# Scaling the compressed branch's weights one head later, and turning them behind the next head's weights

## What is computed

```python
s_c = einsum('bghqd,bgcd->bghqc', qb, k_cmp) + dense_bias(d_c)   # compressed branch
p_c = masked_softmax(s_c, d_c >= 0)                               # 15 weights a query
o_c = einsum('bghqc,bgcd->bghqd', p_c, v_cmp)
# the selected and the window branch have the same form over the 256 keys: o_s, o_w
o = stack([o_c, o_s, o_w])
y = sum(gates[..., None] * o * silu(z), axis=2)                   # over the 3 branches
out = y.reshape(Bn, T, B_WIDTH) @ out_w
```

## Time and profile before

| what | us |
| --- | --- |
| median of 3 runs | 1065.21 |
| lowest and highest of them | 1064.49, 1065.55 |
| the profiled execution, its own time | 1068.07 |
| its span, first to last instruction | 1066.3 |
| TensorE busy in the span | 1024.5 (96%) |
| VectorE busy | 689.1 (65%) |
| ScalarE busy | 624.1 (59%) |
| GpSimd busy | 126.2 (12%) |
| mean granted TensorE clock | 0.994 |

### The profile page before, as it was taken

How to read it: one execution, slowest core, us unless ns; L and a number is a source line. 1 busy time by engine, 2 the same in 40 slices (tenths; PEclk the granted TensorE clock), 3 DMA queues, 4 the chain that set the end, 5 groups by cost and what they waited for, 6 DMA issues and landing times. The chain is left out here.

```text
span 1066.3 us, 16886 instructions
## 1 busy us (share of the span) xinstructions
PE 1024.5 (96%) x6975; PEld 920.6 (86%) x6975; DVE 689.1 (65%) x980; ACT 624.1 (59%) x954; POOL 126.2 (12%) x119
## 2 busy tenths in 40 slices
PE   6999998999999999999999999999999989999997
PEld 5999897988998888689888799999889869899995
DVE  5788676857865687776566564545557876545454
ACT  6679676655664666365666654344456975443443
POOL 1010048440200122530000100000000100000000
PEclk9999999999999999899999999999999999999999
DMA  9885255443677432246332465565544355655540
GB/s 337 301 256 169 77 160 197 150 128 92 198 244 269 159 119 80 80 133 213 129 119 81 137 216 177 182 196 182 177 155 159 122 175 178 196 177 182 196 159 40
DMA packets 117500, 178.41 MB, mean 167 GB/s; under 512 B 5204, under 2 KB 74098, under 8 KB 117424
## 3 DMA queue, kind: packets, MB, share of 16 engines
q1 hardware_dynamic: 116160, 174.23, 50.0%
q0 software_dynamic: 1120, 2.97, 0.8%
q10 hardware_dynamic: 144, 0.13, 0.0%
HBM read 176.27 MB, written 1.05 MB: 166 GB/s over the span
## 5 line engine op out<-in xcount | busy, mean ns | idle before, releaser
L1481 DVE TENSOR_TENSOR sb_w_lo<-sb_raw,sb_w_hi 128x2048 fp32r<-128x2048 f32 (+1 forms) x139 | 309.5, 2227 | 202.1 <-ACT sb_w_hi L775 202.0
L775 ACT ACTIVATE sb_w_hi<-sb_raw 128x2048 fp32r<-128x2048 f32 (+1 forms) x135 | 256.2, 1900 | 136.4 <-PE G L2319 106.3
L2317 PE MATMUL X<-sb_hT_hi,sb_w_hi 128*128 128x256 f32 x784 | 223.2, 285 | 2.6 <-DVE sb_hT_lo L1843 1.1
L2318 PE MATMUL X<-sb_hT_lo,sb_w_hi 128*128 128x256 f32 x784 | 221.3, 282 | 0.0
L2319 PE MATMUL X<-sb_hT_hi,sb_w_lo 128*128 128x256 f32 x784 | 221.2, 282 | 0.0
L2317 PEld LDWEIGHTS X<-sb_hT_hi,sb_w_hi 128*128 128x128 f32 x784 | 149.3, 190 | 5.4 <-DVE sb_w_lo L1481 2.2
L2318 PEld LDWEIGHTS X<-sb_hT_lo,sb_w_hi 128*128 128x128 f32 x784 | 149.4, 191 | 0.7
L2319 PEld LDWEIGHTS X<-sb_hT_hi,sb_w_lo 128*128 128x128 f32 x784 | 149.4, 191 | 0.0
L2317 PE MATMUL G<-sb_w_hi,sb_uT_hi 128*128 128x512 f32 x304 | 121.4, 399 | 4.8 <-DVE sb_uT_lo L2257 4.8
L2319 PE MATMUL G<-sb_w_hi,sb_uT_lo 128*128 128x512 f32 x304 | 120.6, 397 | 0.0
L2318 PE MATMUL G<-sb_w_lo,sb_uT_hi 128*128 128x512 f32 x304 | 120.5, 396 | 0.0
(11 more groups left out here) (507 smaller groups left out, 1970.7 us busy)
## 6 DMA issues: line engine op xcount, KB each, us to landing
sb_raw<-in_mlp_w SPq DMA_DIRECT2D x64, 1024.0 KB, 5.2
sb_raw<-in_ada_w SPq DMA_DIRECT2D x22, 1024.0 KB, 5.3
sb_raw<-in_b_in_w SPq DMA_DIRECT2D x16, 1024.0 KB, 5.7
sb_raw<-in_a_in_w SPq DMA_DIRECT2D x14, 1024.0 KB, 7.0
sb_raw<-in_sb_w_qkv SPq DMA_DIRECT2D x12, 1024.0 KB, 5.2
sb_raw<-in_rg_w_in SPq DMA_DIRECT2D x8, 1024.0 KB, 5.3
sb_raw<-in_a_out_w SPq DMA_DIRECT2D x4, 1024.0 KB, 5.1
sb_raw<-in_b_out_w SPq DMA_DIRECT2D x4, 1024.0 KB, 5.3
```

The costliest lines, as they stand in the source:

```text
L775: nc.scalar.activation(split_tile(w_hi, m)[:, 0:nk * w], raw_of(b)[:, 0:nk * w], ACT.Copy).then_inc(S["w_hi"], 1)
L1481: ins = nc.vector.tensor_tensor(split_tile(w_lo, m)[:, at], raw_of(b)[:, at], split_tile(w_hi, m)[:, at].bitcast(F32), ALU.subtract)
L2317: dt32(out, lh, rh, start=first, stop=False, skip_group_check=shared)
L2318: dt32(out, lh, rl, start=False, stop=False, skip_group_check=shared)
```

## The change

It moves two calls. On VectorE `c_scale()` goes from head 10, behind `scores(12)`, to head 11, behind that head's copy and `z_silu` and ahead of `scores(13)`. On TensorE `c_weights_T()` goes from head 11, behind `scores(13)` and ahead of `head_out(11)`, to head 12, right behind `weights_T(12)` and ahead of `scores(14)`. No instruction is added or removed, and ScalarE's, GpSimd's and SyncE's lists stay as they are.

```diff
--- before.py
+++ after.py
@@ -2049,10 +2049,10 @@
                 nc.vector.tensor_copy(pT[h % 2][:, 1, :], TB[1][:, 0:384]).then_inc(S["pT1"], 1)
                 if h in Z_TILES:
                     z_silu(2 + Z_TILES.index(h))
+                if h == 11:
+                    c_scale()
                 if h + 2 < BH:
                     scores(h + 2)
-                if h == 10:
-                    c_scale()
                 if h in Z_SPLITS:
                     split_for(first_mm["b_z"] + 6 + Z_SPLITS.index(h))
                 if h >= 2 and h % 2 == 0:
@@ -3042,6 +3042,8 @@
             piece = 0
             for h in range(BH):
                 weights_T(h)
+                if h == 12:
+                    c_weights_T()
                 for i in range((Z_PIECES[h] + 1) // 2):
                     z_piece(piece)
                     piece += 1
@@ -3050,8 +3052,6 @@
                 for i in range(Z_PIECES[h] // 2):
                     z_piece(piece)
                     piece += 1
-                if h == 11:
-                    c_weights_T()
                 if h in (12, 13):
                     c_out(h - 12)
                 if h == BH - 1:
```

## The result

The changed kernel takes **1070.23 us** (median of 4 launches, 1068.42 to 1071.02) against 1065.38 before: a ratio of 1.0039, 95% interval 1.0027 to 1.0050. It is slower by 4 to 5 us: the medians are 4.9 apart, the ratio stands for 4.2. I had forecast 1065.8 and a range up to 1067.2; the result lies outside it, on the side of the rival that I had given 0.05.

The account below looks back on a forecast made before the run. It took nmx(13) on VectorE, releasing `scores(14)`, `head_exp(13)` and then `c_out(0)`, to bound the stretch. All terms were 0 except 0.6 us from the port, with the clock unchanged: 1065.8 on the median 1065.21, range 1063.7 to 1067.2.

Parts of the forecast that it names:

- Part 1: VectorE, head 10: with `c_scale` gone, `head_out(11)` on TensorE begins 2.15 us earlier, worth 0 at the end.
- Part 2: VectorE, head 11: `c_scale` enters at 425.78; the work ahead of nmx(13) is the same, in itself 0.
- Part 3: VectorE against GpSimd: L2011 runs into L716, L595 is pushed behind it, and nmx(13) comes 0.6 us late.
- rival C: VectorE against GpSimd: both `c_scale` products lose to L716 and L595, nmx(13) 1.4 us late, 1066.6; chance 0.18.
- Parts 4 to 6: GpSimd's L716 of head 14 ends later, SyncE's DMA goes earlier, TensorE's `c_weights_T` has 1.4 us to spare; each costs 0.
- The clock: TensorE around `c_out(0)`: half clock taken as unchanged, with its 1.90 us on the chain staying.
- rival E: TensorE: the clock falls elsewhere, low also through `head_out(12)` and `weights_T(13)`, 2 us more, 1067.8; chance 0.05.
- The trace I predicted from: Whole kernel: profiled execution of 1068.07 us, 2.86 above the median 1065.21; sum made against it, its difference put on the median.
- Rival B: TensorE: gaps shorter than 2.59 us keep 2.4 GHz, `c_out(0)` gives back 1.90 less 0.6, 1063.9 or 1063.3; chance 0.14.
- The transposes: TensorE's wait: by the skill, transposes filling it don't count as busy the same way; clock stays low, nothing in the sum.

Follow-up runs that it names:

- the second trace: The changed kernel launched again with no edit; median 1070.35 us, ratio 1.0041 against the kernel before.
- filled twice: The changed kernel plus two unused 512-column matmuls on TensorE, one behind `c_weights_T`, one behind `scores(14)`; 1066.19 us, ratio 0.9997 against the kernel before.

## Why the prediction was wrong

*Part 1 (`head_out(11)` 2.15 earlier, worth nothing):* right. It was 2.17, and `c_out(0)` did not move forward.

*Part 2 (VectorE's work ahead of nmx(13) is the same):* right. VectorE stood still nowhere ahead of it.

*Part 3 (the port):* right in mechanism, high in size. I had nmx(13) 0.6 late; it was 0.33, in every trace with this order (8.33 or 8.34 against 7.99 to 8.01). L2010 came first (425.92, 0.02 ahead of L716) and was not held, so rival C did not happen; L2011 was held to the end of L716, and L1949 again ended with the pair L595 (429.14 and 429.12; before 429.95 and 429.92), as I had reckoned. What I charged too much is L595: I let it start only behind L2011, 0.58 late. It started right behind L716, as before, and L2011 ended inside it (427.22), so the pair took 2.34 instead of 2.04, and that 0.30 is what nmx(13) lost.

*Parts 4 to 6:* right. L716 of head 14 took 2.71 at no cost, the DMA went out earlier at no gain, and `c_weights_T` had its time to spare.

*The clock:* this is the step that failed: "I take the clock as unchanged." I had argued that the sum of TensorE's idle time stays, and took it that the half clock would stay with it. The sum did not shrink: 4.39 us in the four gaps, against 2.59 and 0.71, where part of the work between already ran at half speed. But a half clock costs what lies under it. Before, the half clock comes from the one gap of 2.6 us (it is gone when the gap is filled); it begins in the gap or within 2 us of its end, and much of its 6.8 us goes by over matmuls behind which TensorE has a wait; the path pays 0.9 to 1.9. After the change it begins 10.0 us behind nmx(12), and 9.4 in the second trace, instead of 5.2 to 7.5. That is right ahead of `c_out(0)`, where the path runs through TensorE without a gap, and it lasts 10.2 us. The path pays 4.56 in one trace and 4.27 in the other. The difference, 2.4 to 3.7 us, and the port's 0.34 are the local loss: 27.26 and 26.97 at `head_out(15)` against 23.24 and 24.28.

This is rival E, whose place I had right and to which I gave 0.05, because I saw nothing that should move the fall. Its 2 us came on top of what `c_out(0)` already paid in the trace that I had. Against that trace the path pays 2.64 and 2.35 more, so the price was near; it left out `scores(15)` and the start of `c_out(1)`. From `c_out(0)` to `c_out(1)` everything at 1.2 GHz costs 4.1 (8.60-4.47), less the 1.9 already paid.

*The trace I predicted from* was the second step that failed, where I put its difference on the median. It was a launch with the dearer of the two placings of the half clock (1.92 of the path against 0.88), and the median launch is one of the quicker ones. So a rival priced from it was 1.0 us too cheap.

*Rival B (shorter gaps keep the clock up):* did not happen. With shorter gaps the half clock began later, not never. Nor does their length alone set its start: with `c_scale` behind `scores(13)` the longest gap is 2.89 us, and the clock falls 10.0 behind nmx(12) all the same. The orders with the late fall have in common that `head_out(11)` runs early, 3.5 behind nmx(12), behind a wait of only 0.87; no run tests that by itself.

*The transposes:* I had set the Trainium skill's "TensorE: Matmul & The Clock Gate", Part 4 (PE-mode transpose), which has it that a transpose doesn't count as busy in the same way, beside the trace. No run here decides it: `c_weights_T` moved alone changed nothing, but nothing else was held still while the transposes were exchanged for matmuls.

*Where the rest of the 4.9 us is.* Each traced span is a sum of three parts: up to nmx(12), from there to `head_out(15)`, and the rest. Between the first traces of the two kernels that is -1.13, 2.98 and 0.95, which makes the 2.8 between their spans; between the second ones 1.13, 3.73 and -0.06, which makes 4.8. The first part goes by the start of the kernel (last section) and has nothing to do with the change; the third by the half clock near 865 us. An estimate for the medians: the median launch of the kernel before has a mean clock of 0.995, like the trace that pays 0.88, and the slower five of the nine launches of the changed one have 0.990, like the trace with 6.8 us of half clock near 865 us. That gives 3.7 to 4.0 and 0.9, 4.6 to 4.9. It rests on one traced launch of each kind.

What stays open: why the clock stays low for 10.2 us in one order and 6.8 or 3.4 in another, and what sets its fall. A matmul of 0.86 us in either of two waits ahead of `c_out(0)` avoided it here; the runs do not show the rule. Nor do they show whether the change has a part in the longer half clock near 865 us or whether that is chance.

## What to carry to other kernels

Moving TensorE's waits, or splitting one long one into several, isn't neutral even if the chain stays as long: ask where the clock will fall afterwards, and what lies under the half clock. It is cheap over work that is followed by a wait and dear over a run of matmuls on the path. Where TensorE must wait ahead of such a run, a matmul that computes nothing can be worth more than it costs: here 0.86 us of it in a wait gave back 4.6.

A trace is one launch. Before pricing a clock effect from it, compare its time with the median of the launches: here the traced launch was 2.9 us above it, and its half clock cost the path 1.0 more than that of a launch near the median.

A wait that the profile names is not the bound if the engine it names is full: follow the chain on from the wait to what sets the next stage before you count its removal.

## What the runs showed of the hardware that I had not expected

- Adding one matmul of 512 columns (0.86 us at 2.4 GHz) to waits of 1.3 and 1.4 us removed a half-clock stretch of 10.2 us, whichever of two waits it was put in.
- With the same instructions in two orders, the half clock in the attention costs the path 0.9 to 1.9 us in one and 4.3 to 4.6 in the other, while the gap of 3.87 us, the longest tried, went with a half clock of 6.8 us that was over before `c_out(0)` (1.88 long), though it held its start back.
- A VectorE instruction that started 0.02 us before a GpSimd one was not held up, the next one, 0.23 us later, was: 1.07 instead of 0.66.
- A half clock in another stretch of the kernel, near 865 us, was 6.8, 3.4 or 0 us long in launches whose lists are the same there, and cost about 0.9 us where it was 6.8.
- The stretch itself begins between 419.1 and 421.9 us (nmx(12)) in launches of kernels that are the same up to there. It goes with when TensorE gets quick near the kernel's start: in the first trace of before, the matmuls of 256 columns take 0.41 us until 33.5 us and 0.28 from then on, in the trace of the changed kernel filled twice they take 0.28 from 27.9 on, and nmx(12) is at 421.94 and 419.07. Half of the 5.6 us between is 2.8, near the 2.87 between the two nmx(12): in that time the matmuls go at about half pace (they follow each other at 0.21 against 0.12 us). The granted clock reads 1.00 there in both traces, so it is the lengths that show this, and that it is the clock is my reading. In the other twelve traces the change of pace lies between 29.3 and 32.2 and nmx(12) between 419.76 and 421.31. The two timelines, before first:

```profile
33.13 0.41 PE L2318 MATMUL G<-sb_hT_lo,sb_w_hi 128*128 128x256 f32 x1
...
33.55 0.28 PE L2317 MATMUL G<-sb_hT_hi,sb_w_hi 128*128 128x256 f32 x1
```

```profile
27.92 0.28 PE L2318 MATMUL G<-sb_hT_lo,sb_w_hi 128*128 128x256 f32 x1
```

   Single launches of the same kernel therefore differ by some us, and a change of a few tenths can't be read from the times, only from one trace against another.
